# Scaling the probabilities of the banded attention on ACT instead of DVE

## What is computed

```python
# a block of 128 queries sees its own block of keys and the two beside it, |i-j| <= 128; 8 query heads, 2 key heads
s = jnp.einsum('bnqhgd,bnkhd->bnhgqk', qb, kw).astype(jnp.float32) * (HEAD_DIM ** -0.5)
s = jnp.where(valid[None, :, None, None], s, -1e30)
p = jax.nn.softmax(jnp.concatenate([s, sink_col], axis=-1), axis=-1)[..., :-1]
o = jnp.einsum('bnhgqk,bnkhd->bnqhgd', p.astype(v.dtype), vw)
```

## Time and profile before

| | |
|---|---|
| median of three runs | 3252.45 us (3251.24 to 3255.47) |
| the profiled execution: its own time | 3248.34 us |
| its span | 3246.6 us |
| PE busy, of the span | 85% |
| DVE busy | 55% |
| ACT busy | 35% |
| POOL busy | 36% |
| steps of the banded attention, first layer | 222 to 460 us |
| the same, second layer | 1817 to 2056 us |

### The profile page before, as it was taken

One profiled execution on the slowest core, in us unless ns is written; L12 is line 12 of the kernel. 1 busy time (PEld: TensorE's weight loads), 2 busy tenths in 40 slices (PEclk: granted clock), 3 DMA queues, 4 the chain that ended last, 5 costly groups with the idle time before them and its releaser, 6 DMA issues. The chain is left out here.

```text
span 3246.6 us, 39703 instructions
## 1 busy us (share of the span) xinstructions
PE 2770.6 (85%) x15402; PEld 2265.1 (70%) x15402; DVE 1790.6 (55%) x2117; ACT 1120.6 (35%) x1862; POOL 1160.9 (36%) x494
## 2 busy tenths in 40 slices
PE   6978988888879888899888889888887898697996
PEld 4857776677657667777667677677776676586784
DVE  4148646676488462366241676477664882434743
ACT  3123324566345303331110333256563443133211
POOL 4343223222256521055353422322223664102551
PEclk8989999999989998899989999999999999798997
DMA  5242214221344435564233422322213454456431
GB/s 177 78 134 87 72 65 119 78 85 59 102 151 144 150 112 149 174 210 128 71 129 102 126 66 72 114 84 84 72 60 116 161 170 124 125 149 220 154 119 72
DMA packets 393828, 378.40 MB, mean 117 GB/s; under 512 B 90528, under 2 KB 332832, under 8 KB 393632
## 3 DMA queue, kind: packets, MB, share of 16 engines
q1 hardware_dynamic: 356768, 295.02, 30.3%
q10 hardware_dynamic: 36864, 80.75, 6.6%
HBM read 247.70 MB, written 127.99 MB: 116 GB/s over the span
## 5 line engine op out<-in xcount | busy, mean ns | idle before, releaser
L201 PE MATMUL pair<-h_hi,w_hi 128*128 128x512 f32 x1792 | 739.6, 413 | 125.2 <-PEq L132 65.7
L201 PE MATMUL pair<-h_lo,w_hi 128*128 128x512 f32 x1792 | 713.0, 398 | 0.0
L201 PE MATMUL pair<-h_hi,w_lo 128*128 128x512 f32 x1792 | 711.5, 397 | 0.0
L185 POOL TENSOR_TENSOR w_hi<-w_stage,masks 128x1024 fp32r<-128x1024 f32 x108 | 276.2, 2557 | 1012.3 <-PE pair L201 816.4
L201 PEld LDWEIGHTS pair<-h_hi,w_hi 128*128 128x128 f32 x1792 | 346.9, 194 | 238.6 <-SPq L130 68.9
L201 PEld LDWEIGHTS pair<-h_lo,w_hi 128*128 128x128 f32 x1792 | 346.1, 193 | 73.8 <-issue 6.0
L201 PEld LDWEIGHTS pair<-h_hi,w_lo 128*128 128x128 f32 x1792 | 344.9, 192 | 75.4
L187 POOL TENSOR_TENSOR w_lo<-w_stage,w_hi 128x1024 fp32r<-128x1024 f32 x108 | 300.2, 2779 | 8.5
L216 ACT ACTIVATE ev<-pair 128x512 f32<-128x512 f32 x224 | 131.9, 590 | 439.0 <-PE pair L201 438.9
L153 PE MATMUL pair<-h_hi,w_hi 128*128 128x512 f32 x576 | 182.9, 399 | 39.9 <-DVE h_lo L534 26.7
L1289 ACT ACTIVATE diff_p<-pair,diff_stat 128x1024 f32<-128x1024 f32 x128 | 142.8, 1116 | 190.4 <-DVE diff_stat L1384 179.6
(11 more groups left out here) (285 smaller groups left out, 5188.9 us busy)
## 6 DMA issues: line engine op xcount, KB each, us to landing
w_stage<-in_w_in SPq DMA_DIRECT2D x132, 512.0 KB, 4.3
proj<-ev ACTq DMA_DIRECT2D x132, 512.0 KB, 2.7
gate<-proj SPq DMA_DIRECT2D x48, 512.0 KB, 3.6
prep_x<-proj SPq DMA_DIRECT2D x24, 512.0 KB, 3.5
resid<-xT SPq DMA_DIRECT2D x16, 512.0 KB, 8.4
diff_vx<-proj SPq DMA_DIRECT2D x16, 512.0 KB, 3.3
prep_g<-gc_rows SPq DMA_DIRECT2D x16, 512.0 KB, 4.6
qd_t<-prep_eg SPq DMA_DIRECT2D x16, 512.0 KB, 2.6
```

The lines of the kernel that those rows point to most:

```text
L185: nc.gpsimd.tensor_tensor(w_hi[s][:], w_stage[s][:], bcast(ones, KC), ALU.mult).then_inc(q["side_hi"], 1)
L201: last = nc.tensor.matmul(bank(self.banks[half]), a[s][:, c, :], b[:, c, w], start=(c == 0 and n == 0), stop=(c == KC - 1 and n == 2))
```

## The change

ACT multiplies the two heads by the reciprocal, by an activation `Copy` with the reciprocal as its scale of each partition, in place, right behind the Exp of the sink. For that ACT waits on `recip`, the semaphore that DVE raises with L969. DVE no longer waits on `recip` and goes on with `gate_output` or `low_part(n-1)`. `probs` is raised by ACT's second multiplication.

```diff
@@ -868,6 +868,11 @@
                                                  bias=st[:, 1, h:h + 1], accum_out=st[:, 3, h:h + 1])
                         nc.scalar.activation(st[:, 4, :], st[:, 2, :], ACT.Exp).then_inc(q["exped"], 1)
+                        act.wait_ge(q["recip"], START + n + 1)
+                        for h in range(2):
+                            last = nc.scalar.activation(PR[s][:, h, 0:nb * P], PR[s][:, h, 0:nb * P], ACT.Copy,
+                                                        scale=st[:, 6, h:h + 1])
+                        last.then_inc(q["probs"], 1)
                         if n in (0, 1):
                             gate_in(0, n)
@@ -967,11 +972,6 @@
                         nc.vector.reciprocal(st[:, 6, :], st[:, 5, :]).then_inc(q["recip"], 1)
-                        dve.wait_ge(q["recip"], START + n + 1)
-                        for h in range(2):
-                            last = nc.vector.tensor_scalar(PR[s][:, h, 0:nb * P], PR[s][:, h, 0:nb * P],
-                                                           st[:, 6, h:h + 1], None, ALU.mult)
-                        last.then_inc(q["probs"], 1)
                         if n % 2 and n >= 3:
                             gate_output((n - 3) // 2)
```

## The result

The changed kernel takes 3299.7 us (median of 4 runs, 3293.9 to 3301.5), the kernel before 3252.7 us: a ratio of 1.0140 (95% interval 1.0123 to 1.0158), or 46 us (40 to 51). The forecast was 3289 us, with a range of 3266 to 3306. The profiled execution took 3293.9 us, its span is 3292.1. One execution each of e2, e4 and the kernel before beside them took 5537 to 9477 us; the medians and ratios in this text leave these three out.

The account below looks back on a forecast made before the run. PE was taken as near its limit, with short chains over ACT's copy and high part setting the steps. Walk +38.8, L836 and L842 +7, returned delays -9 gave +37 us on 3252.45: 3289 us, range 3266 to 3306.

Parts of the forecast that it names:

- The bound: In the steps: PE near its limit, DVE second; two short chains matter, over ACT's high part and its projection copy.
- The removal: Two multiplications in each of 64 steps leave DVE: 0.67 us a pair, 43 us in all, plus delays under POOL.
- a third of the delays: Of 28 us by which POOL delays DVE's multiplications (L972), a third was taken as returned: -9 us.
- The addition: Two activations of 384 columns on ACT each step: 1.10 us a pair, bounds 0.80 and 1.24; next instruction 1.00 us after its start.
- The walk: Steps 22 to 25 with ACT's new order: cycle 2.15 us longer; 16 cycles with the DMA's part give +38.8 us.
- the share of the DMA: Where the projection copy's DMA falls on step 23, 0.5 us passes to PE, in half the cycles: 8 x 0.55.
- The bare price: Cost of the place in ACT's queue with no delays returned: 38.8 and 7, 46 us.
- The surcharge of L836 and L842: Five steps a layer put these operations, 1.05 us each, behind ACT's scaling: up to +10, taken as +7 us.
- The clock: Later phases just start later; at a granted clock of 0.98 there is nothing to get back from it.
- A: Rival: faster, all 28 us of POOL's delays return and ACT's queue costs nothing; 3224 us, chance 0.07.
- B: Rival: no change, ACT's lateness is covered by PE's projection half of 5.6 us; 3252 us, chance 0.06.
- C: Rival: slower by more; no delay returns (+9), corrections in full (+3), pair 1.24 us (+7); 3308 us, chance 0.09 with nearby cases.

Follow-up runs that it names:

- e2: Kernel before plus one line: ACT waits for the reciprocal where the change puts its multiplication, DVE still multiplies; 3264.6 us, ratio 1.0024.
- e4: Changed kernel with ACT's two multiplications cut to 2 of 384 columns, wait and place kept; 3275.2 us, ratio 1.0057.
- e10: Kernel before with ACT multiplying at the end of its step, behind the projection copy and the high part; 3236.9 us, ratio 0.9948.
- e5: Changed kernel with ACT's multiplication moved behind the projection copy, still ahead of the high part; 3273.2 us, ratio 1.0069.
- e9: Changed kernel with L842 and L836 of five steps a layer put ahead of the multiplication again; 3293.2 us, ratio 1.0114.
- e1: Kernel before without the multiplication by the reciprocal on any engine; the reciprocal is still computed; 3237.9 us, ratio 0.9955.
- e6: Kernel before with POOL's split of the weights cut to one block of 128 of 1024 columns; 3216.9 us, ratio 0.9896.
- e7: Changed kernel with POOL's split of the weights cut to one block of 128 of 1024 columns; 3257.3 us, ratio 1.0016.
- the cut kernels: Kernel before and changed kernel, each with POOL's split of the weights cut to 128 of 1024 columns; 3216.9 and 3257.3 us.
- e8: Changed kernel with about 0.9 us more of ACT copies a step behind the multiplication, ahead of probs; 3353.6 us, ratio 1.0309.

## Why the prediction was right, and where a size was off

**The bound.** Right. Two short chains set the steps, over the copy and over the high part. The runs put more on the high part (39 us from e10 to e5) than on the copy (15 us from e5 to e9).

**The removal.** The 0.67 us a pair is gone from DVE, and doesn't show as such, as predicted. The forecast gave a third of the delays back, 9 us. Without any multiplication (e1) it is 15 us. In the changed kernel nothing comes back on balance (e6, e7). This is the term that was mis-sized: -9 was forecast, +6 measured (-3 to 15). Step 9 shows where it goes. The pair of 4.70 us is gone from it, and still it takes 12.3 us from mask to mask instead of 11.8: two of DVE's small operations, which took 0.16 us each, now take 1.21 and 2.32 us beside POOL, and the one behind the Exps takes 1.90 as before (1.97). The prediction had named this ("stand under it in turn") and yet counted a third as returned. Step 19 shows what was added to it. DVE, in the changed kernel:

```profile
387.24 1.90 DVE L965 SCALAR_TENSOR_TENSOR small<-small 128x2 f32<-128x2 f32 x1
...
389.25 3.38 DVE L910 SCALAR_TENSOR_TENSOR win_zt<-win_zt,win_zx 128x1024 f32<-128x1024 f32 x1
...
392.73 0.17 DVE L974 RECIPROCAL small<-small 128x2 f32<-128x2 f32 x1
```

POOL, ACT and PE at that time:

```profile
389.20 2.35 POOL L187 TENSOR_TENSOR w_lo<-w_stage,w_hi 128x1024 fp32r<-128x1024 f32 x1
```

```profile
392.93 1.12 ACT L873 ACTIVATE win_s<-win_s,small 128x384 f32<-128x384 f32 x2 [2.17 <-DVE small L974]
393.96 0.57 ACT L216 ACTIVATE ev<-pair 128x512 f32<-128x512 f32 x1
```

```profile
394.68 0.77 PE L201 MATMUL pair<-h_hi,w_hi 128*128 128x512 f32 x1 [5.21 <-ACT ev L216]
```

Beside POOL, an operation on the gate takes 3.38 us on DVE instead of 1.22; the reciprocal behind it is late, ACT waits 2.17 us for it, and the copy, whose data PE had ready before 388, starts at 393.96. PE is idle for 5.21 us. In the kernel before, the copy stood behind the Exps alone: a delay of DVE that came between the small operations ahead of the Exps and the reciprocal could not reach the copy of its step. The multiplication is safe from POOL now, but this part of DVE's work has been put into PE's path.

**The addition.** Right within 0.03 us: the pair took 1.12 us in the rows (1.10 forecast, bounds 0.80 and 1.24), the next instruction started 1.03 us after it began (1.00).

**The walk.** Right, and step by step: from mask to mask the four steps took 6.91, 7.41, 7.92 and 8.30 us, where the walk had 6.89, 7.39, 7.91 and 8.24. The cycle is 30.5 us (30.4 forecast), the reciprocal to the low part 1.88 us (1.86), the wait for L216 over 15 us (17.3). But one walked cycle was taken for all sixteen, and that it fits on average is luck: without POOL's long operations the seven four-step cycles from step 2 of the first layer grew by 0.3, 4.1, 3.3, 0.5, 3.8, 2.3 and 2.8 us, 2.4 on average, which is what 2.15 and the share of the DMA give. The bare price was summed as 46 us; the cut kernels differ by 40 (32 to 46), and by 43 in their profiled steps. So this part was some us too dear or right, and its error and that of the delays have opposite signs.

**The surcharge of L836 and L842.** Forecast 7 us; e9 has 6.5 to 8, with an interval that reaches nearly to nothing.

**The clock.** The sentence that there is nothing to get back from the clock was true and beside the point: there was something to lose. From the mask of step 0 to that of step 31, PE's busy time grew by 11.4 and 7.9 us, for all but the same matmuls (1183 records instead of 1178); over the whole kernel, with the same 15402, it grew by 13.0. Around the wait of step 19 (stretch, length, busy PE, PEld, DVE, ACT, POOL, granted clock, DMA share, GB/s):

```profile
389.00:394.60 5.60, 0.47 (x6) 0.14 (x2) 4.17 (x6) 3.00 (x8) 2.47 (x2) 0.78 0.25 58
394.70:398.70 4.00, 4.00 (x10) 3.17 (x11) 2.79 (x4) 0.81 (x1) 0.00 (x0) 0.50 0.82 305
398.70:402.70 4.00, 4.00 (x21) 3.35 (x20) 0.63 (x4) 2.75 (x8) 0.00 (x0) 0.97 0.00 0
```

PE was busy for 0.47 of 5.6 us; in the 4 us that followed, it had the lower of its clock levels (1.2 of 2.4 GHz), and got 10 records of matmuls done, where the next 4 us have 21. So this wait cost more than its length. The kernel before has such places too, after its waits of 4.82 and 3.93 us in the turns (at 305.27 and 364.59). Around the second, and then a stretch with busy DMAs:

```profile
366.90:370.90 4.00, 4.00 (x13) 3.19 (x12) 3.32 (x7) 2.65 (x7) 0.00 (x0) 0.57 0.00 0
...
380.90:384.90 4.00, 3.29 (x21) 2.44 (x20) 2.36 (x7) 2.07 (x7) 0.00 (x0) 1.00 0.80 246
```

So the load of the DMAs doesn't set the clock: here it is 0.57 at a share of 0.00 and 1.00 at a share of 0.80. In the first layer the changed kernel has six waits of PE of over 2 us (2.5 to 5.3), each with a lowered clock behind it. The kernel before has three (3.3 to 4.8), and behind the shortest of them the clock stays at 1.00.

The forecast left this out: the walk priced the waits by their length. How much of the 47 us the clock makes is not shown. PE's busy time is no measure of it alone, since from e6 to e7 it grew as well (by 13.8 us from mask to mask in both layers), while the granted clock fell only from 1.00 to 0.99 and 0.97. Nor do e6 and e7 separate it from POOL's delays, as they take away both the delays and most of the clock's fall.

**The rivals.** A (28 us back) had the right mechanism, but for another kernel: e10 has 17 to 20 us of gain, since there neither the copy nor the high part stands behind the multiplication. B (covered) is refuted by the result, and e2 and e4 show that even the wait with little or no work isn't covered. C (3308) is within 8 us of the result, and its first reason, that no delay returns (+9), is what e6 and e7 show; its others are not: the pair took 1.12 us and not 1.24, and e9 gives no sign of more than 7 us or so for L842 and L836. With its 3299.7 us, the result lies nearer to C than to the forecast of 3289.

## What to carry to other kernels

Before work is moved to an engine that is idle on average, look at what stands behind it in that engine's queue and who waits for that; here the same two instructions cost 47 us in one place and gain 17 to 20 us at the end of the same step. A new wait can bring the delays of the engine waited for into the queue of the one that waits, as in step 19. Put such work behind what others wait for, and ahead only of what itself comes later.

## What the runs showed of the hardware beyond this

- After 5.2 us in which PE waited, its granted clock was 0.50 for some 4 us and 0.97 after that. In the steps of the first layer as a whole, it went from 0.98 (kernel before) to 0.93 (changed) and 0.91 (e8, the longest waits), and up to 1.00 in e6.
- A multiplication of 384 columns by a value a partition took 0.61 us on ACT, as long as an Exp of the same tile, against 0.37 us on DVE; beside POOL, DVE's took up to 4.70 us for a pair, ACT's pair no more than 1.12 us in the rows shown.
- An operation of 1024 columns with both inputs in SBUF took 3.38 us on DVE beside one of POOL, where all eight of its kind took 1.22 us at most in the kernel before. Operations of 2 columns were held up as well: 2.32 us beside POOL in step 9 of the changed kernel, against 0.16.
